# Scan tables of an S5 layer built by GpSimd from pre-turned rows instead of by VectorE and TensorE

## The reference, cut to what matters

```python
def _s5_direction(u_ctx, u_lat, lam, dt, bmat, cmat):
    lam_dt = lam * dt[:, None]
    lam_bar = jnp.exp(lam_dt)
    b_bar = ((lam_bar - 1.0) / lam)[..., None] * bmat
    powers = jnp.exp(lam_dt[None] * jnp.arange(1, S5_CHUNK + 1)[:, None, None])
    def step(h, u_chunk):
        bu = jnp.einsum('btgs,gps->btgp', u_chunk.astype(jnp.complex64), b_bar)
        ...
        y = jnp.einsum('btgp,gsp->btgs', xs, cmat).real
```

## Time and profile before

| | |
|---|---|
| runs | 1574.93, 1572.53, 1574.73 us; median 1574.73 |
| profiled execution | span from first to last instruction 1571.2 us; this is the only time recorded of it, so what lies around its span is read as the 3.5 us to the median |
| TensorE | busy 1503.4 us, 96% of the span |
| VectorE, ScalarE, GpSimd | busy 872.9, 402.3, 565.2 us |
| DMA | 273 MB, 174 GB/s on average |

### The profile page before, as it was taken

The page is one execution under the profiler, slowest core; times in us unless marked ns, Lnnn a source line. Parts: engine busy times, 40 slices in busy tenths (PEclk is TensorE's granted clock), DMA queues, the critical chain, the costliest instruction groups (busy, mean ns, idle before and its releaser), DMA issues.

```text
span 1571.2 us, 25477 instructions
## 1 busy us (share of the span) xinstructions
PE 1503.4 (96%) x10192; PEld 1129.3 (72%) x10192; DVE 872.9 (56%) x1745; ACT 402.3 (26%) x956; POOL 565.2 (36%) x412
## 2 busy tenths in 40 slices
PE   4999989999999999999998999999999999999998
PEld 3455555666655558898877888887788874688887
DVE  5979944554578978378466321243543422265642
ACT  1222243333311222322233011001223550232210
POOL 4013340000002314101002977773496301477774
PEclk9999999999999999999999999999999999999999
DMA  9856771050286646747666455445544133455441
GB/s 332 221 173 194 242 237 45 3 159 14 100 262 228 202 174 180 273 166 287 251 252 260 159 195 182 161 163 185 191 167 146 70 108 107 131 179 164 168 150 68
DMA packets 172605, 272.99 MB, mean 174 GB/s; under 512 B 51405, under 2 KB 85304, under 8 KB 171208
## 3 DMA queue, kind: packets, MB, share of 16 engines
q1 hardware_dynamic: 146096, 201.08, 38.1%
q0 software_dynamic: 16512, 42.49, 8.4%
q10 hardware_dynamic: 9880, 27.78, 4.8%
HBM read 228.26 MB, written 42.99 MB: 173 GB/s over the span
## 4 chain that ended last, share of the span: by engine, by line
PE 88%; DVE 5%; DMA 3%; issue 2%; ACT 2%; POOL 0%; DVEq 0%; ACTq 0%; POOLq 0%
PE bank L499 82%; PE bank L502 6%; DMA memory<-in_w_mod 1%; DMA memory<-mc_scratch 1%; DVE memory L2417 1%; DVE memory L2418 1%; DVE memory L2424 0%; DVE memory L2421 0%; DMA memory<-in_s_log_dt 0%; DVE memory L2574 0%; ACT memory L1514 0%; ACT memory L1386 0%; ACT memory L1738 0%; DVE memory L2445 0%; DVE memory L2444 0%
## 5 line engine op out<-in xcount | busy, mean ns | idle before, releaser
L499 PE MATMUL bank<-memory 128*128 128x256 f32 (+8 forms) x9244 | 1404.7, 355 | 40.4 <-issue 8.5
L499 PEld LDWEIGHTS bank<-memory 128*128 128x128 f32 (+4 forms) x9244 | 1022.3, 166 | 378.1 <-issue 250.1
L2783 POOL DMA_DIRECT2D mc_scratch<-memory x32 | 28.0, 874 | 505.5 <-DVE memory L2138 447.7
L502 PEld LDWEIGHTS bank<-memory 128*128 128x128 f32 (+1 forms) x948 | 109.3, 142 | 59.4 <-issue 33.6
L502 PE MATMUL bank<-memory 128*128 128x128 f32 (+1 forms) x948 | 125.9, 277 | 23.5 <-ACT memory L1358 8.6
L2822 POOL TENSOR_TENSOR memory<-memory 128x1024 f32<-128x1024 f32 (+1 forms) x34 | 80.9, 2378 | 143.5 <-PE bank L499 96.2
L2808 POOL DMA_DIRECT2D memory<-mc_scratch x32 | 17.3, 541 | 189.7 <-PE bank L499 189.7
L2824 POOL TENSOR_TENSOR memory<-memory 128x1024 f32<-128x1024 f32 (+1 forms) x34 | 80.9, 2380 | 2.7
L2789 POOL DMA_DIRECT2D k_scratch<-memory x128 | 76.2, 629 | 14.5 <-ACT memory L1431 14.1
L2827 POOL TENSOR_TENSOR memory<-memory 128x1024 f32<-128x1024 f32 (+1 forms) x34 | 80.0, 2353 | 2.7
L2825 POOL TENSOR_TENSOR memory<-memory 128x1024 f32<-128x1024 f32 (+1 forms) x34 | 80.4, 2366 | 0.0
(11 more groups left out here) (305 smaller groups left out, 1284.3 us busy)
## 6 DMA issues: line engine op xcount, KB each, us to landing
memory<-in_s_w_glu SPq DMA_DIRECT2D x32, 1024.0 KB, 7.5
memory<-in_w_mod SPq DMA_DIRECT2D x12, 2048.0 KB, 14.1
memory<-in_w_ffn_up SPq DMA_DIRECT2D x22, 1024.0 KB, 6.9
memory<-in_w_in SPq DMA_DIRECT2D x10, 2048.0 KB, 8.0
mc_scratch<-memory POOLq DMA_DIRECT2D x32, 512.0 KB, 4.5
mb_scratch<-memory ACTq DMA_DIRECT2D x32, 512.0 KB, 3.7
memory<-mb_scratch SPq DMA_DIRECT2D x32, 512.0 KB, 7.3
memory<-mc_scratch POOLq DMA_DIRECT2D x32, 512.0 KB, 6.5
```

Source lines behind the costliest of these rows:

```text
L499: return nc.tensor.matmul(o, l, r, start=start, stop=stop, skip_group_check=free)
L502: return nc.tensor.transpose(o, i, ident[0:n, 0:n])
L2783: pool.dma_start(mc_dram[u], over(mc[:, u % 3, GS:GS + 1], (144, 8), (1, P))).then_inc(*S.up("mc_out%d" % (u % 3), u, by=16))
```

## The change: what it does

It takes the mb half out of `unit(u)` and all of `unit_turned(u)` away. Instead:

- the raw b of each quarter q (8 units) is turned once by TensorE (`b_turned(q)`, 8 transposes, four quarters, all in the head and gates stages), copied by ScalarE and stored to `bt_scratch`;
- VectorE computes the pole powers with their scale as rows (`power_rows`, 31 small instructions, after unit 2); GpSimd stores them to `pw_scratch`;
- for each unit SyncE loads a **pair** (`pair_load(u)`: 16 rows of `bt_scratch` repeated over 128 partitions, 512 KB, and two pieces of 256 KB of `pw_scratch` with each row repeated 16 times) into half of ring slot 1, which the ring no longer uses until the last out0 load. GpSimd multiplies it in `mixed_unit(u)`: two TENSOR_TENSOR of 128x1024, two of 128x4x128, and a store to `mb_scratch`. Units 0 to 26 are built in the memory of `gtb` (`mixed_b[0]`), units 27 to 31 in that of hT. Pair u waits for the products of unit u-2;
- the pair loads stand in SyncE's queue between the weight loads. All six `mod_product(1, ct)` lie in heads 8, 9, 11, 12, 14 and 15 and use ring slot 2 one after the other;
- `gate_rows(0)`, which writes `gtb`, moves behind the last head on TensorE and ScalarE; ScalarE first waits there for the stores of units 25 and 26;
- the stores of mc tables and taps move from GpSimd's queue to ScalarE's; the four multiplications of `norm(h)` move from VectorE to ScalarE.

```diff
-MOD_AT = {3: 0, 5: 1, 10: 2, 12: 3}
+MOD_AT = {8: (1, 0), 9: (1, 1), 11: (1, 2), 12: (1, 3), 14: (1, 4), 15: (1, 5)}
+LAST_MIXED = 5
...
+        pairs = ring[:, 1, :].rearrange("p (a b n) -> p a b n", a=2, b=2)
+        mixed_b = (gtb, hT_flat[:, 0:2048].rearrange("p (a n) -> p a n", a=2))
...
-            def unit_turned(u):
...
+            def b_turned(q, i):
+                pe.wait_ge(*S.at("b_load%d" % (q % 2), q))
+                for ql in range(2):
+                    b = bank(pe, ("bT", q, ql), [("bT", (q, ql))], i + ql)
+                    for n in range(4):
+                        c = (n % 2) * 512 + (n // 2) * 256 + ql * P
+                        last = tr(b[:, n * P:(n + 1) * P], b_loaded(q)[:, c:c + P])
+                    last.then_inc(*S.up("bT_mm", (q, ql)))
...
@@ TensorE, behind the gates
             mod_turned(0, 5, 7)
-            gate_rows(0)
-            unit_turned(15)
+            kernels(7)
...
@@ TensorE, behind the heads
-            mod_product(1, 4)
-            mod_product(1, 5)
-            mod_turned(1, 4)
-            mod_turned(1, 5)
+            gate_rows(0)
             for ql in range(2):
                 c_turned(2, ql, 7)
...
@@ ScalarE, unit_stored
+                act.wait_ge(*S.at("mc", u))
+                act.dma_start(mc_dram[u], ...).then_inc(*S.up("mc_out%d" % (u % 3), u, by=16))
                 if u % 2:
...
+                    for j in range(L):
+                        act.dma_start(to, kt[:, kp % 2, (7 - j) * GS:(7 - j) * GS + P]).then_inc(*S.up("k_out%d" % (kp % 2), kp, by=16))
...
@@ ScalarE, behind the heads
+            for u in (NU - LAST_MIXED - 2, NU - LAST_MIXED - 1):
+                act.wait_ge(*S.at("mb_out%d" % (u % 2), u))
+            gate_rows(0)
             for ql in range(2):
                 c_conjugated(2, ql)
...
@@ GpSimd
+            def mixed_unit(u):
+                b, w, o = pairs[:, u % 2, 0, :], pairs[:, u % 2, 1, :], mixed_b[u >= NU - LAST_MIXED][:, u % 2, :]
+                both = lambda v, c=0, s=P: over(v[:, c:c + 1], (2 * P, 4), (s, 2), (1, P))
+                part = lambda v, c: over(v[:, c:c + 1], (2 * P, 4), (1, P))
+                pool.wait_ge(*S.at("pair_in%d" % (u % 2), u))
+                if u >= 2:
+                    pool.wait_ge(*S.at("mb_out%d" % (u % 2), u - 2))
...
+                nc.gpsimd.tensor_tensor(both(o), both(b), both(w, 0, 0), ALU.mult).then_inc(*S.up("mix_op", (u, 0)))
+                nc.gpsimd.tensor_tensor(both(w), both(b, P, -P), both(w, P, 0), ALU.mult).then_inc(*S.up("mix_op", (u, 1)))
+                nc.gpsimd.tensor_tensor(part(o, 0), part(o, 0), part(w, 0), ALU.subtract).then_inc(*S.up("mix_op", (u, 2)))
+                nc.gpsimd.tensor_tensor(part(o, P), part(o, P), part(w, P), ALU.add).then_inc(*S.up("mixed", u))
+                pool.dma_start(mb_dram[u], o).then_inc(*S.up("mb_out%d" % (u % 2), u, by=16))
...
@@ SyncE
+            def pair_load(u):
+                q, g8 = u // 8, u % 8
+                if u >= 2:
+                    sp.wait_ge(*S.at("mixed", u - 2))
...
+                sp.dma_start(b, dview(bt_dram, q * P * 8 * P + g8 * GS * 8 * P, (0, 8), (8 * P, GS), (1, 8 * P)))
+                for ql in range(2):
+                    src = dview(pw_dram, (16 * q + 8 * ql + g8) * 4096, (512, 8), (0, GS), (1, 512))
+                    sp.dma_start(w[:, ql * 512:(ql + 1) * 512], src)
...
+            pair_loads(0, 11)
+            ring(("mod", 1, 0))
...
+            ring(("mod", 1, 4))
+            pair_loads(20, 22)
             ring(("out0", 0, 0))
+            ring(("mod", 1, 5))
+            pair_loads(22, 24)
             ring(("out0", 0, 1))
             sp.wait_ge(*S.at("k_mm", H - 1))
-            b_load(3)
+            b_again(3)
+            pair_loads(24, 28)
             ring(("out0", 1, 0))
+            pair_loads(28, NU)
             c_load(3)
             ring(("out0", 1, 1))
```

More of the change, by code:

```diff
@@ L615, in _ @@
                         c_turned(0, ql, 2 + ql)
+                    b_turned(0, 0)
             for n in range(16):
@@ L623, in _ @@
                 last.then_inc(*S.up("gate_mm", n))
-                if n >= 2:
-                    unit_turned(n - 2)
+                if n >= 3 and n % 2:
+                    kernels((n - 3) // 2)
+                if n in (6, 10, 12):
+                    b_turned({6: 1, 10: 2, 12: 3}[n], 4)
                 if n == 5:
@@ L1527, in _ @@
                     head(h + 1)
+                if h == 0:
+                    norm(h)
                 if h >= 1:
@@ L2181, in _ @@
                     V.tensor_copy(kr[:, t, 1, :], k_r).then_inc(*S.up("kr", t))
-            for u in range(2, 6):
+            unit(2)
+            power_rows()
+            for u in range(3, 6):
                 unit(u)
@@ L2791, in _ @@
-            for half in range(2):
-                for u in range(16 * half, 16 * half + 16):
-                    c_store(u)
-                    if u % 16 >= 4 and u % 2 == 0:
-                        taps_store((u - 4) // 2)
-                for kp in (8 * half + 6, 8 * half + 7):
-                    taps_store(kp)
+            pool.wait_ge(*S.at("power_rows"))
+            for dr in range(2):
+                e = 1 - 2 * dr
+                to = dview(pw_dram, (7 * 512 if dr == 0 else 0) + dr * 256, (4096, P // 2), (-512 * e, 8), (1, 2 * P))
+                pool.dma_start(to, over(ptab[64 * dr:64 * dr + 64, 0, 0, 0:1], (2 * P, 8), (1, 2 * P))).then_inc(*S.up("pw_out", by=16))
@@ L2799, in mc_load @@
+            for u in range(NU):
+                mixed_unit(u)
             def mc_load(u0, u1):
```

272 lines of the change are left out of this document (156 added, 116 removed).

## The result

The changed kernel takes **1694.8 us** (median of 4 runs, 1691.9 to 1695.8) against 1574.1 for the kernel before beside it: ratio 1.077, 95% interval 1.0754 to 1.0784. I had forecast 1597.5 and a range of 1580 to 1620. The sign was right; the loss is 120.7 us where I had put 22.8, five times as much.

What follows compares the result with a forecast made beforehand. TensorE was taken to bound gates, attention and out0. Terms up to out0's start summed to +25.0, with the later ones to +22.8: span 1571.2 becomes 1594.0, plus 3.5 for the runs' median gives 1597.5 us, range 1580 to 1620.

Steps and rivals of the forecast that it cites:

- Transposes gone, the wait at half clock behind the gates, `kernels(7)` earlier: Up to attention: fewer TensorE transposes and a wait with lowered clock, `kernels(7)` ending at 204.5, 15.9 us earlier.
- Eight tap stores of about 0.33 us, 0 to 1 us in sum: On ScalarE behind `kernels(7)` and unit 31: the stores cost 0 to 1 us, taken as 1.
- GpSimd's clock of 8.3 us: GpSimd building tables: each unit takes 8.3 us, its products and the issue of its store; 32 units are 266 us.
- Pair 0 at about 220: Start of GpSimd's units: the first pair is loaded at about 220 us, after the up-projections and the uq load.
- pair loads of 2.7 us of queue time: SyncE's pair loads: each 1 MB pair takes 2.7 us of queue time.
- rival 3: Pair loads repeating DRAM rows take 5.4 us; GpSimd restarts, c load and out0 turns are later: 1605 to 1620, chance 0.26.
- The mod loads: Modulation weight loads in attention: mod 5 lands at 418, some 3 us after head 15 asks; +2.9 us.
- The new wait at bank 7: End of attention: TensorE waits for ScalarE's gate-row copy, held by the stores of units 25 and 26; +32.8 us.
- Half clock behind that wait (+3.3) and behind the c load (+1.6): In out0: TensorE runs at half clock after idling, +3.3 us at the start and +1.6 behind the c load.
- The c load in out0: Behind tile 7 of out0: the c load, issued after pair 31, comes at about 540, +5.0 us.
- VectorE and GpSimd taking turns: In out0: products from SBUF alternate, a VectorE unit taking some 10 us; costed at nothing, up to 10 us without cover.
- Rival 1: End of attention: the tables are in time, out0 starts at 438.7, and the kernel takes 1551 us; chance 0.07.

Runs made afterwards that it cites:

- e1: The changed kernel with the tap stores of kernels 0 to 7 back on GpSimd's queue: 1679.6 us.
- e4: The kernel before, with only the stores of mc tables and all taps issued by ScalarE: 1618.1 us.
- e8: The kernel before, with only the 32 mc table stores issued by ScalarE, the taps staying with GpSimd: 1582.4 us.
- e2: The changed kernel with pair loads of outermost size 16 instead of 8, same bytes, other numbers in the tables: 1637.1 us.
- e7: The changed kernel with pair loads reading 128 different rows, same bytes, other numbers in the tables: 1628.4 us.
- e12: e9 with all taps on GpSimd, layer 1's modulation products spread over more heads, and b loaded as eight loads of 16 rows: 1600.0 us.
- e14: e12 with five of six modulation loads cut to an eighth of their bytes, part of the modulation other numbers: 1574.4 us.
- e9: The changed kernel with taps 0-7 on GpSimd, modulation loads by ScalarE, pw_scratch rows twice, SyncE reordered, units 24-31 in hT: 1622.2 us.

## Why the prediction was wrong, point by point

In one sentence: the chain that I forecast was there, but a pair load cost far more than I gave it, on every pair and on the weights beside it, and the tap stores on ScalarE's queue, which I had put at 1 us, cost 15 (e1).

- **Transposes gone, the wait at half clock behind the gates, `kernels(7)` earlier** (-15.9): right. With the taps off ScalarE (e1) it is -14.3, and the clock behind the wait there is 0.53, 0.50, 0.50 and 0.76 in the four windows of 2 us from 202 to 210.
- **Eight tap stores of about 0.33 us, 0 to 1 us in sum**: this term failed. They took 5 to 12.6 us a time, and with the two waits of 9 us and half clock behind them (mean clock 0.69 from 139.6 to 146, 0.52 from 229.8 to 236) the first row of the table is +8.6, 24.5 off. I took the issue time of a 512 KB table store for that of the taps, though the same taps had cost GpSimd 0.6 us each before, and I did not ask who waits behind ScalarE. e1 shows it, and e4 less e8 in the kernel before.
- **GpSimd's clock of 8.3 us**: right, 8.27 to 8.28 in e2, e7 and e12. But it was not the limit of the change as made. **Pair 0 at about 220** was 236.5; **pair loads of 2.7 us of queue time** were 5.4 to 6.8, by an estimate from 1 MB and the 194 to 154 GB/s of the windows, and in the heads 9.7 us and more from the last issue to the use. That is my rival 3 in its number (5.4 us, it says), at a chance of 0.26 and a price of 8 to 23 us; what it names beside the number, the repeated rows, is at most the 6 to 9 us between e2 and e7, and the outermost size is the rest. The price is the step that failed: I added it to a few restarts of GpSimd, where it acts on every pair, since pair u waits for unit u-2 and each pair is then later than GpSimd wants it, and I gave the weights nothing of it. e2 and e7 measure both together: 58 to 66 us of the 98 that I was off.
- **The mod loads**: I let one of six be 3 us late. Three were, by 38.7 us. That is the same step: e7 keeps their place in the queue and the bytes around them, and its waits in the heads are 4.0 us. "Queues 21% busy, there is room" held for the bytes of wide loads, not for loads that ran at 154 to 194 GB/s ahead of a ring with one slot for six weights. In the mended versions the weights are late again (22.6 us in e12); e14 takes most of their bytes away and is 25.6 us faster than e12, but how much of that is ScalarE as their issuer was not measured.
- **The new wait at bank 7**: right in place, releaser and cause; 49.7 us instead of 32.8, since it inherits every delay of the tables and loses what delays the heads. That it came out within 17 us is luck: TensorE got there at 506.3, not 437.0, and ScalarE's copy came at 555.2, not 469.8, 69 and 85 us late. e9 removes the wait.
- **Half clock behind that wait (+3.3) and behind the c load (+1.6)**: no run shows either term apart. The runs show the stretches: TensorE is back at 556.0 and the clock is 0.50 in the windows from 556 to 562 and 0.66 from 562 to 564; behind the c load it is back at 637.8, with 0.50 from 638 to 644 and 0.68 from 644 to 646. At half speed that would be some 3.7 and 3.8 us, an estimate from these windows., from which the 3.3 came, has the clock, not the time lost.
- **The c load in out0** (+5.0): right in place, behind pair 31 in SyncE's queue; 14.0 us. In e2, with the wide loads, it is 6.7.
- **VectorE and GpSimd taking turns**, costed at nothing: small in the change, where one wait of 4.3 us is VectorE's. In the mended kernel it is my reading of out0, where TensorE's eight microseconds less gain nothing in e14: the products are stretched and TensorE waits 8.7 us for VectorE. No run took the sharing away.
- **Rival 1, tables in time and 1551 us**: e14 meets its condition and gives 1574. Even there I would have been 23 us off. The trace has a mod wait, waits for ScalarE and VectorE in the heads, and the turns in out0 for it; their shares were not measured apart.

What stays open: how the 14 us that attention gives back in e14 divide between ScalarE's norm and half clock was not measured apart; nor was a form tried in which the tables' second half is built away from out0, or one with wide loads in which SyncE issues the modulation weights in the mended order. The move of `norm` from VectorE to ScalarE was never run by itself. No version here beats the kernel before.

## What to carry to other kernels

Price a moved DMA at its issue time for that very shape, on the queue that it goes to, and list what stands behind it there: on ScalarE's queue the series of eight small stores cost some 33 us in e4, the 512 KB stores beside them 10. Look at the outermost size of a load's access pattern before its bytes; two pairs of numbers swapped were worth 58 us, and the kernel with the wide loads (e7) moved more bytes a second from head 0 on, 242 GB/s against 201, and waited 4.0 us for weights in the heads against 38.7. And where a queue's loads wait for an engine which waits for those loads, a delay per round is paid in every round (two units of 9.2 us each at the start of the changed kernel, 8.27 in e2), and by everything else in that queue.

## What the runs showed that I had not expected

- On ScalarE's queue the same eight tap stores took 4.96 us beside 80 to 174 GB/s of traffic and up to 12.6 beside some 350, while GpSimd issued them at 0.6 us each: 603 ns on average and 849 at most over 128 of them in e12.
- Half of the 2 MB modulation loads landed over 17.7 us after their issue in the changed kernel (14.1 in the kernel before), and over 10.3 us in e7, at the same DMA share of 0.70 from head 0 on.
- Eight loads of 64 KB (3.8 us of issuing) served GpSimd better than one of 512 KB (0.6): pitch 8.28 us in e12 against 8.8 over the first ten units of e9, whose other loads are the same.
